# Splitting the operands of the branch and mixing projections in a two-block kernel on one Trainium2 core

## The reference, cut to what matters

Two network blocks follow each other over 256 tokens (batch 1) of width 1024. The first is a mixer of retention and gated delta rule, with a feed-forward part behind it; the second (an RWKV-7 mixer and causal attention) is not touched. The part of the first block that matters here:

```
        do = gated_delta_chunkwise(cq, ck, cv, g, beta)
        do = do * lax.rsqrt(jnp.mean(do * do, axis=-1, keepdims=True) + EPS) * dn_norm_g[l]
        do = do.reshape(B, T, DN_V) * jax.nn.silu(dz)
        y_dn = do @ w_dn_br[l]

        merged = jax.nn.sigmoid(gate_r) * y_ret + jax.nn.sigmoid(gate_d) * y_dn
        h = h + merged @ w_o[l]

        u2 = rmsnorm(h, g_ffn[l])
        up = causal_dwconv(u2 @ w_up[l], ffn_conv_w[l]) + ffn_conv_b[l]
```

## Time and profile before

| | us |
|---|---|
| median of 3 executions | 1555.76 (1553.38 to 1556.97) |
| the profiled execution | 1557.62 |
| its span in the profile | 1555.8 |
| PE busy | 1502.9 (97%) |
| PE weight loads busy | 1327.2 (85%) |
| DVE busy | 982.4 (63%) |
| ACT busy | 843.3 (54%) |
| POOL busy | 49.1 (3%) |

### The profile page before, as it was taken

The page is one execution under the profiler, slowest core; times in us unless marked ns, Lnnn a source line. Parts: engine busy times, 40 slices in busy tenths (PEclk is TensorE's granted clock), DMA queues, the critical chain, the costliest instruction groups (busy, mean ns, idle before and its releaser), DMA issues.

```text
span 1555.8 us, 26754 instructions
## 1 busy us (share of the span) xinstructions
PE 1502.9 (97%) x10508; PEld 1327.2 (85%) x10508; DVE 982.4 (63%) x1881; ACT 843.3 (54%) x2045; POOL 49.1 (3%) x28
## 2 busy tenths in 40 slices
PE   7999999999999999898899999999999999999997
PEld 7599877887889999797798888988889887789986
DVE  3368386444348885687677777777777413666764
ACT  3256444445147775555666666666665414555553
POOL 1144100000000000000000000000000000000000
PEclk9999999999999999999999999999999999999999
DMA  9364232212445555322111101111011125333331
GB/s 374 115 227 163 92 108 87 77 55 82 135 161 179 179 187 190 108 96 95 55 55 55 52 32 55 55 56 51 32 56 55 54 89 206 126 109 122 123 121 43
DMA packets 25820, 167.79 MB, mean 108 GB/s; under 512 B 3680, under 2 KB 5088, under 8 KB 6112
## 3 DMA queue, kind: packets, MB, share of 16 engines
q1 hardware_dynamic: 24512, 164.97, 29.9%
q10 hardware_dynamic: 1184, 1.11, 0.2%
HBM read 165.03 MB, written 1.05 MB: 107 GB/s over the span
## 4 chain that ended last, share of the span: by engine, by line
PE 88%; ACT 5%; DVE 4%; issue 2%; DMA 1%; SPq 0%; DVEq 0%; ACTq 0%
PE bank L747 8%; PE bank L748 8%; PE bank L749 8%; PE bank L731 5%; PE bank L1089 4%; PE bank L1072 4%; PE bank L877 3%; PE bank L823 3%; PE bank L1239 3%; PE bank L1223 3%; PE bank L1102 3%; PE bank L1074 2%; PE bank L1073 2%; PE bank L761 2%; PE bank L1216 1%
## 5 line engine op out<-in xcount | busy, mean ns | idle before, releaser
L660 DVE TENSOR_TENSOR ring_lo<-ring,w_hi_rw 128x1024 fp32r<-128x1024 f32 x117 | 142.6, 1221 | 39.0 <-ACT w_hi_rw L1503 37.8
L1503 ACT ACTIVATE w_hi_rw<-ring 128x1024 fp32r<-128x1024 f32 x117 | 122.6, 1051 | 52.3 <-PE bank L749 31.3
L660 DVE TENSOR_TENSOR w_lo<-ring,w_hi 128x1024 fp32r<-128x1024 f32 x80 | 98.3, 1232 | 76.2 <-ACT w_hi L1503 75.3
L1072 PE MATMUL bank<-x_hi,w_hi_rw 128*128 128x272 f32 x384 | 135.4, 352 | 0.1
L1471 ACT ACTIVATE arena<-bank 128x272 f32<-128x272 f32 (+2 forms) x165 | 66.8, 406 | 125.4 <-PE bank L749 37.8
L1503 ACT ACTIVATE w_hi<-ring 128x1024 fp32r<-128x1024 f32 x98 | 103.2, 1056 | 21.0 <-PE bank L749 15.0
L1074 PE MATMUL bank<-x_hi,ring_lo 128*128 128x272 f32 x384 | 110.9, 289 | 0.0
L1073 PE MATMUL bank<-x_lo,w_hi_rw 128*128 128x272 f32 x384 | 110.9, 289 | 0.0
L747 PE MATMUL bank<-u_hi,w_hi 128*128 128x256 f32 x320 | 90.8, 284 | 1.4 <-DVE w_lo L660 1.4
L748 PE MATMUL bank<-u_lo,w_hi 128*128 128x256 f32 x320 | 90.5, 283 | 0.0
L749 PE MATMUL bank<-u_hi,w_lo 128*128 128x256 f32 x320 | 90.5, 283 | 0.0
(11 more groups left out here) (488 smaller groups left out, 4304.7 us busy)
## 6 DMA issues: line engine op xcount, KB each, us to landing
ring<-wstream SPq DMA_DIRECT2D x151, 1024.0 KB, 4.9
con<-consts SPq DMA_DIRECT2D x1, 2400.0 KB, 15.2
h<-xT SPq DMA_DIRECT2D x1, 1024.0 KB, 6.2
arena<-wlora ACTq DMA_DIRECT2D x1, 1024.0 KB, 4.6
out<-arena SPq DMA_DIRECT2D x4, 256.0 KB, 2.5
arena<-decays SPq DMA_DIRECT2D x2, 384.0 KB, 5.6
gain_post<-gains SPq DMA_DIRECT2D x1, 512.0 KB, 5.7
arena<-decays SPq DMA_DIRECT2D x1, 256.0 KB, 5.7
```

What stands on the lines that cost most here:

```text
L660: ops.tensor_tensor(lo, whole, hi.bitcast(F32), ALU.subtract).then_inc(S(signal), 1)
L1072: nc.tensor.matmul(b[:, 0:T2], w_hi, x_hi[:, x, k, :], start=k == 0, stop=False)
L1503: nc.scalar.activation(hi, whole, ACT.Copy).then_inc(S("w_hi_ready"), 1)
```

## The change

Branch outputs 2 to 7 and all mixing outputs go through `project_split`. Their 14 units are put into `unit_start` between the first ones and those of the up projection (`mix_end` is the end of them). Their high parts lie in an area of their own (`w_hi_mix`), their low parts in the ring, over the weights, so their chunks are still freed by `proj_done`. The activations get parts of their own: `dn_hi`, `dn_lo` for each pair of heads (`round_dn` on ACT, `lower_dn` on DVE, 512 columns each), `mg_hi`, `mg_lo` for each tile of gr. Some counters of the rows of the delta rule are merged into two (`rows_by_act`, `rows_by_dve`), with the same order of work.

```
+        unit_start += list(range(int(starts[78]), int(starts[92]), UB))
+        mix_end = len(unit_start)
...
+            if first_units <= i < mix_end:
+                return whole, w_hi_mix[:, i % HALVES, :], ring_lo[:, at:at + UB * P], unit_start[i] // CB
...
+                in_place = last is not None and first_units <= unit_at.get(last * CB, 0) < mix_end
+                if last is not None and last * CB in unit_at and unit_at[last * CB] < ffn_end and not in_place:
...
+            pe.wait_ge(S("mix_lo_ready"), 4)
             for _m in range(6):
-                project(lambda k: conv[:, 16 + k, :], DT, T1)
+                project_split(dn_hi, dn_lo, DT)
             for m in range(DT):
-                project(lambda k: gr[:, k, :], DT, T1, None if m else "merged")
+                project_split(mg_hi, mg_lo, DT, None if m else "mix_lo_ready", 4)
...
+                        split_hi(down_units(b) if base else min(first_units + 6 + b + HALVES, mix_end))
                         take(outs[:, b, :])
...
+            def round_dn(g):
+
+                act.wait_ge(S("dn_gated"), g + 1)
+                nc.scalar.activation(dn_hi[:, 2 * g:2 * g + 2, :], conv[:, 16 + 2 * g:18 + 2 * g, :], ACT.Copy).then_inc(S("mix_hi_ready"), 1)
...
                     if l == 5:
                         dn_tokens(g)
+                    if g == 3 and l <= HALVES:
+                        split_hi(first_units + l)
+                    if g >= 1 and l == 5:
+                        round_dn(g - 1)
                     dn_take(dn_fill_end(g, f"delta{l}"))
...
-            taken_n[0] += 8
-            act.wait_ge(S("merged"), 8)
+            round_dn(3)
+            for b in range(8):
+                taken_n[0] += 1
+                split_hi(first_units + max(b - 2, 0) + HALVES)
+                act.wait_ge(S("merged"), b + 1)
+                nc.scalar.activation(mg_hi[:, b, :], gr[:, b, :], ACT.Copy).then_inc(S("mix_hi_ready"), 1)
...
+            def lower_dn(g):
+
+                dve.wait_ge(S("mix_hi_ready"), g + 1)
+                V_.tensor_tensor(dn_lo[:, 2 * g:2 * g + 2, :], conv[:, 16 + 2 * g:18 + 2 * g, :],
+                                 dn_hi[:, 2 * g:2 * g + 2, :].bitcast(F32), ALU.subtract).then_inc(S("mix_lo_ready"), 1)
...
+                    if g >= 1 and l == LEVELS - 1:
+                        lower_dn(g - 1)
+                    if g == 3 and l in (3, 5):
+                        split_both(first_units + (l - 1) // 2)
...
             dn_gate(3)
+            split_both(first_units + 3)
+            lower_dn(3)
...
                 V_.tensor_tensor(gr[:, b, :], gr[:, b, :], gd[:, b, :], ALU.add).then_inc(S("merged"), 1)
+                split_both(first_units + max(b - 2, 0) + HALVES)
+                dve.wait_ge(S("mix_hi_ready"), 4 + b + 1)
+                V_.tensor_tensor(mg_lo[:, b, :], gr[:, b, :], mg_hi[:, b, :].bitcast(F32), ALU.subtract).then_inc(S("mix_lo_ready"), 1)
...
-                    if base:
-                        split_both(down_units(b))
+                    split_both(down_units(b) if base else min(first_units + 6 + b + HALVES, mix_end))
```

More of the change, by code:

```diff
@@ L49 @@
 AT_OM = 9824
+AT_W_MIX = 27224
 UP_EARLY = 4
@@ L356, in build @@
         with ExitStack() as over_arena:
+            part("up_to_merged", [P, AT_QK], F32)
+            mg_hi, mg_lo = part("mg_hi", [P, DT, T1]), part("mg_lo", [P, DT, T1])
+            dn_hi = part("dn_hi", [P, DT, T1])
+            part("up_to_w_hi_mix", [P, AT_W_MIX - AT_SCORES], F32)
+            w_hi_mix = part("w_hi_mix", [P, HALVES, UB * P])
+        with ExitStack() as over_arena:
+            part("up_to_dn_lo", [P, 6216], F32)
+            dn_lo = part("dn_lo", [P, DT, T1])
+        with ExitStack() as over_arena:
             part("arena_start", [P, FFN_END], F32)
@@ L672, in _ @@
                     sp.dma_start(gain_post[:, :], gains).then_inc(S("vec_loaded"), 16)
-                if last is not None and last * CB in unit_at and unit_at[last * CB] < ffn_end:
+                in_place = last is not None and first_units <= unit_at.get(last * CB, 0) < mix_end
+                if last is not None and last * CB in unit_at and unit_at[last * CB] < ffn_end and not in_place:
                     sp.wait_ge(S("w_lo_even"), unit_at[last * CB] // 2 + 1)
@@ L852, in _ @@
                 ret_fill(f"v{g}")
-            pe.wait_ge(S("rows_ready"), 1)
+            pe.wait_ge(S("rows_by_dve"), 3)
             for j, (r, c) in enumerate(((0, 0), (0, 1), (2, 0), (2, 1), (3, 0), (4, 1))):
@@ L1522, in take_for_sum @@
                             .then_inc(S("hg_ready"), 1)
-                split_hi(first_units + 2)
+                split_hi(mix_end + 2)
                 norm_root(T1, D)
@@ L1596, in _ @@
                     nc.scalar.activation(rows[0:8, 1, :], bank[2][0:8, 0:T1], ACT.Identity, bias=V("dt_bias", 0, 8))\
-                        .then_inc(S("row_y"), 1)
-            act.wait_ge(S("row_abs"), 1)
+                        .then_inc(S("rows_by_act"), 1)
+            act.wait_ge(S("rows_by_dve"), 1)
             link(nc.scalar.activation(rows[0:8, 5, :], rows[0:8, 5, :], ACT.Exp))
             nc.scalar.activation(rows[0:8, 5, :], rows[0:8, 5, :], ACT.Ln, bias=1.0)
-            nc.scalar.activation(sd[0:8, 0:1], V("a_log", 0, 8), ACT.Exp).then_inc(S("row_ln"), 1)
+            nc.scalar.activation(sd[0:8, 0:1], V("a_log", 0, 8), ACT.Exp).then_inc(S("rows_by_act"), 1)
             ret_took = [0]
@@ L1620, in _ @@
                     conv_silu(2)
-            act.wait_ge(S("rows_g"), 1)
+            act.wait_ge(S("rows_by_dve"), 2)
             nc.scalar.activation(rows[0:8, 3, 0:CH], rows[0:8, 3, 0:CH], ACT.Exp)
-            nc.scalar.activation(rows[0:8, 4, :], rows[0:8, 2, :], ACT.Exp).then_inc(S("rows_exp"), 1)
+            nc.scalar.activation(rows[0:8, 4, :], rows[0:8, 2, :], ACT.Exp).then_inc(S("rows_by_act"), 1)
             for g in range(4):
@@ L1759, in _ @@
             for m in range(2, FT):
-                n = first_units + 2 * m - UP_EARLY
+                n = mix_end + 2 * m - UP_EARLY
                 split_hi(n + 3)
@@ L2236, in rows_abs @@
             def rows_abs():
-                dve.wait_ge(S("row_y"), 1)
+                dve.wait_ge(S("rows_by_act"), 1)
                 link(V_.tensor_scalar(rows[0:8, 5, :], rows[0:8, 1, :], -1.0, None, ALU.mult))
                 link(V_.tensor_tensor(rows[0:8, 5, :], rows[0:8, 5, :], rows[0:8, 1, :], ALU.min))
-                V_.tensor_scalar(rows[0:8, 1, :], rows[0:8, 1, :], 0.0, None, ALU.max).then_inc(S("row_abs"), 1)
+                V_.tensor_scalar(rows[0:8, 1, :], rows[0:8, 1, :], 0.0, None, ALU.max).then_inc(S("rows_by_dve"), 1)
             def rows_decay():
-                dve.wait_ge(S("row_ln"), 1)
-                dve.wait_ge(S("row_abs"), 1)
+                dve.wait_ge(S("rows_by_act"), 2)
+                dve.wait_ge(S("rows_by_dve"), 1)
                 link(V_.tensor_tensor(rows[0:8, 1, :], rows[0:8, 1, :], rows[0:8, 5, :], ALU.add))
@@ L2431, in _ @@
             add_to_h(conv, 68 + 16, 0)
-            split_both(first_units + 2)
+            split_both(mix_end + 2)
             norm([u[:, t, 0:T1] for t in range(DT)], [h[:, t, META:] for t in range(DT)],
```

10 lines of the change are left out of this document (4 added, 6 removed).

## The result

| | before | after |
|---|---|---|
| median of four executions each, on one chip | 1554.57 us (1553.36 to 1556.97) | 1547.78 us (1547.06 to 1548.38) |
| ratio after to before, 95% interval | | 0.9950 (0.9937 to 0.9963) |
| profiled execution | 1557.62 us | 1548.26 us |
| its span, mean granted clock | 1555.8 us, 0.992 | 1546.5 us, 0.993 |

6.8 us less by the medians.

The account below looks back on a forecast made before the run. PE, busy 97% of the span, was taken to bound the kernel. 8.0 - 1.8 - 0.26 - 0.45 = 5.5 us less gave 1550.3 us against the median of 1555.76, range 1547.8 to 1554.8.

Parts of the forecast that it names:

- the last one of the sum: Whole kernel: 5.5 us less, 1557.62 to 1552.1 us profiled; the shown median lies 1.86 lower, so 1550.3 us.
- PE's pace: Branch outputs 2 to 7 and mixing projection: 112 blocks at 0.360 instead of 0.431 us, 8.0 us saved.
- The head: Start of the branch: two low parts on DVE after the last gating delay output 2, costing 1.8 us.
- The delta rule: Step 5 of pairs 1 to 3: ACT's added rounding costs 0.15 us each, 0.45 us; unit splits cost nothing.
- Mixing start and table load: First mixing output: PE waits 0.26 us for mg_lo; ACT's root table load, 1.28 us, stays hidden with 0.6 to spare.
- Rival 2: Mixing projection: the table load costs more than its row, PE waits 0.8 us; 1551.1 us, chance 0.07.
- Queues: Weight loads in branch and mixing: same DMAs in the same order, 183 GB/s needed, no cost.
- Rival 1: Branch outputs 3 to 7: DVE's turn outlasts PE's output, 2.9 us comes back; 1553.2 us, chance 0.10.
- Rival 3: Delta rule does not absorb added work, up to 9.5 us: 1554.6 us at half (chance 0.07), 1559.3 whole (0.04).
- Rival 4: Branch and mixing matmuls: a block takes three quarters of float32 time, 0.324 us; 1546.2 us, chance 0.03.
- Rival 5: Branch and mixing: in-place low parts slow PE's reads, a block stays at 0.431 us; 1558.3 us, chance 0.02.
- Rival 6: Start of the branch and delta rule cost nothing: 7.7 us less, 1548.0 us, chance 0.05.

Follow-up runs that it names:

- the one with a wait of 1.97: Changed kernel with the unit for branch output 2 split behind step 6 of the last pair instead of behind the last gating: 1546.62 us, ratio 0.9949.

## Why the prediction was nearly right and where it failed

Over the four groups of experiments 92 executions of the kernel before have a median of 1555.5 us, and the 25 of them above a mean clock of 0.992 one of 1553.2 us; the changed kernel's 19 (with the first four), all above 0.992, have 1547.5 us. At a like mean clock the change is worth 5.8 us, and the sum said 5.5. The other 2.2 us would be clock in the kernel before. This rests on a choice of executions by their mean clock: none of the 25 was profiled, and that they lack the fall near 1300 us is inferred.

- **The failed step is the last one of the sum**: "The profiled execution took 1557.62 us and would take 1552.1. The median shown, 1555.76, lies 1.86 lower, so against it I predict 1550.3 us." It carries the base over as if all of it stayed. In all three profiles of the kernel before the base held a fall near 1300 us, in which 12 matmuls took 5.78 us instead of 2.99, and in three of the four profiles of the changed kernel this 2.8 us is gone; in the remaining one 1.6 us of it is there. Near 645 us 1.0 us went in the same manner: from the last matmul of the down projection to the first of the rwkv projections 66.8 to 67.0 us pass in the three profiles of the kernel before, 65.9 to 66.0 in three of the changed kernel and 67.3 in its third. The mean clock of 0.992 stood on the page; which stretches lost it, and whether they depend on when they come, was not asked. The range had no case for it and ended 0.02 us too high.
- **PE's pace**: 0.360 a block was taken, 0.353 is right (three times 0.1178), so 0.078 saved a block and 8.7 us, not 8.0. The profile had the number: the outputs of 272 columns with low parts in the ring took 0.125 a matmul, which scaled to 256 columns is 0.118. I read that row as the slower bound and did not scale it; the row with the same columns had its operands in the other place.
- **The head**: 1.66 us by DVE's timeline against 1.82, the mechanism as forecast. Not forecast was the slow clock behind the longer wait (2.32 us against 0.62 before). It costs 1.5 us: from the first to the last matmul of dn_hi the fourth profile of the changed kernel takes 18.1 us, the third, without the fall, 16.6. Five of the eight profiles of kernels with this wait of 2.32 us show it, and so does the one with a wait of 1.97.
- **The delta rule**: right in place, 0.27 to 0.28 us a pair against 0.15, so 0.8 instead of 0.45. The rows gave ACT's lateness; left out was that the four matmuls which wait for it (L941, now L959) then take 0.71 us instead of 0.61. The unit split behind step 3 of the last pair makes DVE's next mask 0.34 us late and the one behind it is on time again, so the units cost nothing, as said.
- **Mixing start and table load**: the first mixing output takes 3.06 us where 24 matmuls at PE's pace take 2.83, so 0.2 us against 0.26. Behind the load the next operation starts after 1.30 us, as in the earlier trace rows, and PE never waits: cover as forecast. The Trainium skill's drain of about 1380 ns behind the load (ScalarE: Activation LUTs, What ACT_TABLE_LOAD costs) is not in the trace here either. Rival 2 falls.
- **Queues**: 140 and 172 GB/s in the two stretches and no wait for a chunk: right.
- **Rival 1** falls: DVE's turn fits, its gatings come 2.81 us apart, at PE's pace. **Rival 3** falls but for the 0.8 us. **Rival 4** and the rule beside it: 0.353 of 0.431 is 0.82; by the four passes of the Trainium skill (FP8 and Floating Point Precision, TensorE Precision Notes) it would be 0.75, so the rule gives the direction and overstates the gain. **Rival 5** falls, and its supposed reason is the reverse of what was measured: low parts in the ring are read faster. **Rival 6** falls: both costs it leaves out are there. That its 1548.0 us lies nearest to the measured 1547.78 is luck: what it saved by leaving out two costs came in fact from the clock.

The balance of the terms as measured is 8.7 - 1.7 - 0.8 - 0.2 = 6.0 us, and 4.5 with the fall at the head; the 5.8 us measured at a like clock lies between them. The mean clock does not see the 1.0 us near 645 us, where both kernels have a fall of one length; without it 4.8 us are left, near the balance with the fall at the head. That the sum of 5.5 came so near is in part luck as well: the saving was set 0.7 us too low, and the fall at the head and the delta rule, 1.5 and 0.35 us, take more than that back.

## What to carry to other kernels

Before a saving is set against a measured time, look in the table of stretches for those where the granted clock is below full. What they lose is part of the base but not of the work, and an edit elsewhere that shifts them can give it back or take it, here with 4 us and with 0.6: count it as a term of either sign, and widen the range by it. A wait that grows on PE is priced at its added length and at the slow matmuls that may follow, here 1.7 + 1.5 us. Scale a row of the trace by its columns before it becomes a bound. And take several executions of the kernel before in its own right: three did not show its two groups.

## What the runs showed of the hardware

- The same wait of PE is followed by a full, a partial or no fall of the clock: 2.81 us of idle time and then 12 matmuls in 5.78 (4 profiles), 4.43 to 4.64 (4) or 2.99 us (10). Executions with a mean clock of 0.992 or less are 22 of 27 in the kernel before and 2 of 11 with 40 extra matmuls ahead; they are 0 of 11 and 9 of 11 in two kernels that differ by eight matmuls.
- Matmuls of 256 columns on rounded operands follow each other 0.1200 us apart when a third of their weights lie in an area of their own and 0.1178 when these lie in the ring. The place of the low parts, with the release of chunks that goes with it, is worth 2.9 us of 180.
- A table load occupied ACT for 1.28 us and the next operation came 0.02 us after it.
- A doubled first matmul of 272 columns, paced at 0.125 us elsewhere, lengthened the stretch by 0.085 to 0.10 us, with PE's idle time nearly unchanged.
